# A packed expert table and a rolled expert loop in a two-layer mixture-of-experts kernel

## The reference

```python
_, top_e = lax.top_k(masked, TOP_K)                      # best group of 4 experts, then 2 of its 4
gates = sum over the two of one_hot(top_e, 16) * weight
a = jnp.einsum('bld,edf->blef', h, w1)                   # D 1024 -> 256 for each expert
g = jnp.einsum('bld,edf->blef', h, w3)
hid = jax.nn.silu(a) * g * gates[..., None]
return jnp.einsum('blef,efd->bld', hid, w2)              # 256 -> 1024, summed over experts
```

## Time and profile before

| what | value |
|---|---|
| time, median of 3 runs | 1067.43 us (1067.35 to 1070.24) |
| the profiled execution: time, span | 1068.16 us, 1066.3 us |
| mean granted TensorE clock | 0.886 |
| busy: PE, weight load (PEld) | 800.7 us (75%), 514.3 us (48%) |
| busy: DVE, ACT, POOL | 345.6, 213.9, 123.0 us |
| chain that ended last | PE 60%, DVE 13%, issue 10%, DMA 5% |

### The profile page before, as it was taken

One profiled execution on the slowest core, in us unless ns is written; L12 is line 12 of the kernel. 1 busy time (PEld: TensorE's weight loads), 2 busy tenths in 40 slices (PEclk: granted clock), 3 DMA queues, 4 the chain that ended last, 5 costly groups with the idle time before them and its releaser, 6 DMA issues.

```text
span 1066.3 us, 14079 instructions
## 1 busy us (share of the span) xinstructions
PE 800.7 (75%) x4044; PEld 514.3 (48%) x4044; DVE 345.6 (32%) x756; ACT 213.9 (20%) x513; POOL 123.0 (12%) x181
## 2 busy tenths in 40 slices
PE   4899998789980797867509999977899528987810
PEld 2675554457860353534208655544577514454500
DVE  1102103842757122111064021046527642221126
ACT  1310003542010122222124000044510001222210
POOL 0310100010120010012044000000001110011021
PEclk9999998999975799989758999989999559998965
DMA  9952493783254977897275422328420368569441
GB/s 379 367 219 87 161 415 136 282 354 118 88 209 177 356 242 271 339 386 285 63 286 220 157 80 79 118 70 322 193 79 11 129 241 340 192 220 349 164 142 63
DMA packets 39840, 223.63 MB, mean 210 GB/s; under 512 B 5008, under 2 KB 5840, under 8 KB 22832
## 3 DMA queue, kind: packets, MB, share of 16 engines
q1 hardware_dynamic: 19008, 155.50, 37.6%
q0 software_dynamic: 12240, 50.22, 13.3%
q10 hardware_dynamic: 8480, 16.33, 4.3%
HBM read 194.70 MB, written 27.33 MB: 208 GB/s over the span
## 4 chain that ended last, share of the span: by engine, by line
PE 60%; DVE 13%; issue 10%; DMA 5%; PEld 5%; ACT 3%; PEldq 2%; POOL 1%; ACTq 1%; POOLq 0%; DVEq 0%; SPq 0%
PE psum L499 18%; PE psum L629 7%; PE psum L638 7%; PE psum L496 6%; PE psum L584 4%; PE psum L670 3%; PE psum L659 3%; PEld psum L584 3%; DMA big<-in_weights 3%; PE psum L616 3%; PE psum L448 2%; PE psum L604 2%; DMA shared<-moe_rows,ridx 1%; DVE mxs L1211 1%; PE psum L462 1%
## 5 line engine op out<-in xcount | busy, mean ns | idle before, releaser
L499 PE MATMUL psum<-big 128*128 128x384 f32 x576 | 190.9, 488 | 2.7 <-issue 2.7
L499 PEld LDWEIGHTS psum<-big 128*128 128x128 f32 x576 | 108.6, 190 | 78.6 <-issue 8.3
L638 PE MATMUL psum<-big,shared 128*64 128x256 f32 x576 | 77.4, 428 | 33.3 <-issue 33.3
L1508 DVE TENSOR_SCALAR shared<-shared 128x128 f32<-128x128 f32 (+1 forms) x28 | 7.0, 251 | 258.1 <-ACT shared L1014 258.1
L584 PE MATMUL psum<-big 128*128 128x256 f32 x384 | 83.9, 380 | 2.0 <-ACT big L951 1.8
L629 PE MATMUL psum<-big,shared 128*128 128x512 f32 x160 | 79.6, 656 | 6.3 <-issue 4.0
L584 PEld LDWEIGHTS psum<-big 128*128 128x128 f32 x384 | 72.6, 190 | 12.9 <-issue 3.2
L638 PEld LDWEIGHTS psum<-big,shared 128*64 128x64 f32 x576 | 51.9, 155 | 54.7 <-issue 41.4
L496 PE MATMUL psum<-big 128*128 128x256 f32 x288 | 68.9, 400 | 7.6 <-DMA big<-in_weights 3.9
L448 PE MATMUL psum<-const,big 128*128 128x128 f32 x160 | 31.4, 308 | 51.4 <-ACT big L841 28.0
L496 PEld LDWEIGHTS psum<-big 128*128 128x128 f32 x288 | 57.1, 201 | 18.1 <-ACT big L848 7.5
(11 more groups left out here) (217 smaller groups left out, 912.6 us busy)
## 6 DMA issues: line engine op xcount, KB each, us to landing
big<-in_weights SPq DMA_DIRECT2D x80, 1024.0 KB, 6.9
big<-in_experts SPq DMA_DIRECT2D x22, 2048.0 KB, 11.4
big<-in_experts SPq DMA_DIRECT2D x22, 1024.0 KB, 8.6
moe_rows<-ln_b POOLq DMA_DIRECT2D x3, 3584.0 KB, 25.4
moe_rows<-shared ACTq DMA_DIRECT2D x20, 256.0 KB, 5.9
moe_rows<-shared ACTq DMA_DIRECT2D x36, 128.0 KB, 6.8
ln_b<-in_ln POOLq DMA_DIRECT2D x4, 1024.0 KB, 6.3
gate_b<-mod_rows POOLq DMA_DIRECT2D x4, 1024.0 KB, 7.3
```

The source lines that it names most:

```text
L499: ins = pe.matmul(bank(name)[:, 0:T], w[piece][:, k, part * P:(part + 1) * P], hT[:, k, :], start=(k == 0), stop=(k == KC - 1))
L638: ins = pe.matmul(psD[HALF * j:HALF * j + HALF, 0:DE], xT[:, k * P:k * P + HALF], w[:, 2 * DE * k + DE * j:2 * DE * k + DE * j + DE], star ...
```

## The change

- The start, full and end tables become one number for each expert in use, `end + 4*full + 16*blocks + 64*start` (T_CODE). PE reads one number a stage, SP's buffer waits take it apart too. Unused places hold only a start, so their end is 0.
- PE's sixteen written-out stages become a loop over turns of four stages (one for each weight buffer). Each stage is nested in the one before it and is entered only if the one before it was in use; an expert's further blocks go through one inner loop for full and half blocks. Each turn reads two codes at its start.
- Experts are taken in the order of their number, those in use first. Layer 0 becomes H H FH H, FF H H H, F F H H, H (four turns); layer 1 becomes H H H H, FFF FFH H H, H (three turns).
- DVE: the ops of rank and of blocks by rank go, others for the place of an expert in use come; four ops and the first block's number move ahead of reading the counts; the index is read before the packed table is built, and the table is ready after it.
- POOL: it takes the first block's number from a small tensor of its own (`from_block`), and the first gather is issued directly on the index, without waiting for the table and without the column copy. The loop goes on from the second block.
- SP reads its expert numbers ahead of the waits, ACT reads one packed flag for this block and the one before.

```diff
 # SP
+first_two = [expert(L, r) for r in range(2)]
+for r in range(2):
+    load_up(first_two[r], r)
...
+    e = expert(L, r)
     if r >= BUFS:
-        used = sp.value_load(tabu[0:1, T_START + r - BUFS + 1:...], ...)
+        used = sp.value_load(tabu[0:1, T_CODE + r - BUFS + 1:...], ...) // 64
         sp.wait_ge(up_full, used)
 # PE
-def expert_table(r):
-    load = lambda at, low, high: pe.value_load(tabu[0:1, at + r:at + r + 1], min_val=low, max_val=high)
-    return load(T_START, 1, BLOCKS * DEPTH + 1), load(T_FULL, 0, TILES), load(T_END, 0, 2)
+def expert_code(turn, q):
+    return pe.value_load(tabu[0:1, bass.ds(turn * BUFS + (T_CODE + q), 1)], min_val=0, max_val=MOST)
...
+def stage(L, turn, q, code, end_before):
+    loads = L * (E // BUFS) + turn
+    end, full_blocks = code % 4, code // 4 % 4
+    blocks, start = code // 16 % 4, code // 64
+    w = expert_buffer(q)
+    def down_before():
+        last_down((q - 1) % BUFS, loads + (q > 0), end_before, start)
...
+    with pe.If(end > 0):
+        pe.wait_ge(up_in[q], loads * 16 + 16)
+        up_block(start, full_blocks)
+        following = expert_code(turn, q + 1) if q < BUFS - 1 else None
+        with pe.Fori(0, blocks) as j:
+            i = start + j
+            tokens_T(L, i + 1)
+            with pe.If(j > 0):
+                pe.wait_ge(down_in[q], loads * 16 + 16)
+                down_full_block(i, w)
+            with pe.Else():
+                down_before()
+            with pe.If(full_blocks - j > 0):
+                hidden_T_full(i)
+            with pe.Else():
+                hidden_T_half(i)
+            with pe.If(blocks - j > 1):
+                up_block(i + 1, full_blocks - j - 1)
+        if q < BUFS - 1:
+            stage(L, turn, q + 1, following, end)
+    with pe.Else():
+        down_before()
...
-table, end = expert_table(0), None
-for r in range(E):
-    table, end = stage(L, r, table, end)
+turns = (pe.value_load(tabu[0:1, T_ACTIVE:T_ACTIVE + 1], min_val=1, max_val=E) + (BUFS - 1)) // BUFS
+with pe.Fori(0, turns) as turn:
+    before = expert_code(turn, -1)
+    stage(L, turn, 0, expert_code(turn, 0), before % 4)
+end = expert_code(turns, -1) % 4
 last = pe.value_load(tabu[0:1, T_LAST:T_LAST + 1], min_val=2, max_val=BLOCKS * DEPTH + 1)
-last_down(L, E - 1, end, last)
+last_down(BUFS - 1, L * (E // BUFS) + turns, end, last)
 # ACT
-before, half_block = block_kind(j - 1), block_kind(j)
+half_block, before = block_kinds(j)          # one load, % 2 and // 2
 # DVE, ahead of the counts
+link(dve.tensor_copy(tab[:, T_FIRST:T_FIRST + 1], tab[:, T_LAST:T_LAST + 1]))
+dve.tensor_copy(from_block[:, 0:1], tab[:, T_FIRST:T_FIRST + 1]).then_inc(from_ready, 1)
+# four ops of 3x16 (t16, v16(13)), moved here from behind the first blocks
 # DVE, who and blocks
-link(tt(grid(0, E, 6), cols(tokens, 6), steps, ALU.is_gt)); link(dve.tensor_reduce(halves, ...))
-link(stt(key, ...)); link(tt(grid(0, E, E), rows(key, E), cols(key, E), ALU.is_gt))
-link(dve.tensor_reduce(rank, grid(0, E, E), AX.X, ALU.add))
+link(ts(active, tokens, 0.0, None, ALU.is_gt))
+link(tt(grid(0, E, E), prev, rows(active, E), ALU.mult))
+link(dve.tensor_reduce(place, grid(0, E, E), AX.X, ALU.add))
+link(stt(place, place, 1.0, active, ALU.add, ALU.mult))
...
-link(tt(grid(0, E, E), grid(1, E, E), rows(halves, E), ALU.mult))
-link(dve.tensor_reduce(by_rank, grid(0, E, E), AX.X, ALU.add))
...
-link(tt(grid(0, E, E), grid(1, E, E).rearrange("p r e -> p e r"), rows(base, E), ALU.mult))
-link(dve.tensor_reduce(first_block, grid(0, E, E), AX.X, ALU.add))
...
-link(tt(two, ..., ALU.mult))                  # 2x2x48, then its sum
+link(tt(slots, ..., ALU.mult))                # 2x48, then its sum
 # DVE, behind sel_ready
-# ten ops of the three tables, table_ready, then the index
+# two sums (T_ACTIVE, T_COUNT), the index into gidx (two ops),
+# then halves (two ops), the code (eight ops), by place (two ops of 256),
+# T_LAST, idle places, table_ready
 # POOL
-await_read(pool, L, "index")
+pool.wait_ge(from_ready, L + 1)
+first = pool.value_load(from_block[0:1, 0:1], min_val=1, max_val=BLOCKS * DEPTH + 1)
+def first_gather(b):
+    pool.wait_ge(xT_full, first + L)
+    await_read(pool, L, "index")
+    pool.indirect_dma_start(xg[b], None, h2_d[:, :],
+                            bass.IndirectOffsetOnAxis(gidx[:, 0:1], 0)).then_inc(xg_in[b], 16)
...
 pool.wait_ge(table_ready, L + 1)
-first = pool.value_load(tabu[0:1, T_FIRST:T_FIRST + 1], ...)
 count = pool.value_load(tabu[0:1, T_COUNT:T_COUNT + 1], min_val=1, max_val=BLOCKS)
-with pool.Fori(0, count + 1) as j:
+with pool.Fori(1, count + 1) as j:
```

More of the change, by code:

```diff
@@ L688, in last_down, with up_block @@
                     with pe.Else():
-                        down_full_block(after, expert_buffer(r))
+                        down_full_block(after, expert_buffer(q))
                     stop_here(pe, "pe")
[L692 to L701, removed]
+            def stage(L, turn, q, code, end_before):
[5 more added lines that the diff above has]
+                    last_down((q - 1) % BUFS, loads + (q > 0), end_before, start)
+                def up_block(i, left):
+                    with pe.If(left > 0):
+                        up_full_block(L, i, w)
+                    with pe.Else():
+                        up_half_block(L, i, w)
@@ L1474, in _ @@
-                link(tt(tab[:, T_FULL:T_FULL + E], blocks, half_last, ALU.subtract))
-                link(stt(tab[:, T_END:T_END + E], by_rank, 0.0, half_last, ALU.is_gt, ALU.add))
-                link(dve.tensor_copy(tab[:, T_FIRST:T_FIRST + 1], tab[:, T_LAST:T_LAST + 1]))
-                link(ts(tab[:, T_START:T_START + E], base, tab[:, T_FIRST:T_FIRST + 1], None, ALU.add))
+                await_product(dve, L, "index")
+                src = bank("index")[:, 0:2 * COLS]
+                link(dve.tensor_copy(rt[:, 10, 0:COLS], src[:, COLS:2 * COLS]))
@@ new lines, in _ @@
+                read_out(tt(gidx[:, :], src[:, 0:COLS], rt[:, 10, 0:COLS], ALU.add), "index")
+                link(tt(grid(0, E, 6), cols(tokens, 6), steps.broadcast_to([P, E, 6]), ALU.is_gt))
+                link(dve.tensor_reduce(halves, grid(0, E, 6), AX.X, ALU.add))
+                link(stt(half_last, blocks, 2.0, halves, ALU.mult, ALU.subtract))
+                link(stt(code, base, 4.0, blocks, ALU.mult, ALU.add))
+                link(stt(halves, blocks, 1.0, half_last, ALU.mult, ALU.subtract))
@@ new lines, in _ @@
+                link(stt(code, code, 4.0, halves, ALU.mult, ALU.add))
+                link(stt(halves, active, 1.0, half_last, ALU.mult, ALU.add))
+                link(stt(code, code, 4.0, halves, ALU.mult, ALU.add))
+                link(ts(st[:, 6:7], tab[:, T_FIRST:T_FIRST + 1], 64.0, None, ALU.mult))
+                link(ts(code, code, st[:, 6:7], None, ALU.add))
+                link(tt(grid(0, E, E), grid(1, E, E), rows(code, E), ALU.mult))
+                link(dve.tensor_reduce(tab[:, T_CODE:T_CODE + E], grid(0, E, E), AX.X, ALU.add))
@@ L1478, in _ @@
                 link(tt(tab[:, T_LAST:T_LAST + 1], tab[:, T_FIRST:T_FIRST + 1], tab[:, T_COUNT:T_COUNT + 1], ALU.add))
+                link(ts(st[:, 7:8], tab[:, T_LAST:T_LAST + 1], 64.0, None, ALU.mult))
+                link(ts(idle, num[:, 0:E], tab[:, T_ACTIVE:T_ACTIVE + 1], st[:, 7:8], ALU.is_ge, ALU.mult))
+                link(tt(tab[:, T_CODE:T_CODE + E], tab[:, T_CODE:T_CODE + E], idle, ALU.add))
                 link(dve.tensor_copy(tabu[:, 0:T_WHO], tab[:, 0:T_WHO]))
                 dve.sem_inc(table_ready, 1)
-                await_product(dve, L, "index")
```

143 lines of the change are left out of this document (59 added, 84 removed).

## The result

The changed kernel takes 1061.9 us against 1067.4 us in the median of 20 runs each; the ratio of the runs is 0.9943, 95% interval 0.9928 to 0.9958. Timed again beside the experiments it was 1059.8 us against 1069.0 us, 0.9927 (0.9893 to 0.9962). So it is faster, by 6 to 8 us after these ratios, inside the stated range and on the forecast side, where I had forecast 16 us.

A forecast was written before the change was run, and what follows sets the result against it. PE was taken to bound both loops, losing mostly to issue, and DVE the stretch ahead. Front -5.4, layer 0's loop -9.5 and layer 1's -1.3 sum to -16.2 us, giving 1051.3 us; range 1038 to 1092.

The forecast's parts named there:

- The bound: Both expert loops: PE is the limit, losing mostly to issue, 30.2 us in layer 0 and 18.4 in layer 1.
- the reading of the long gaps: PE's loops: gaps of 4.3 to 5.1 us are waits for instruction pieces, as stage-end branches skip past fetched code.
- Three changes of turn: ... 3.9 us each: Layer 0's loop: each costs 0.9 us, two reads at up to 1 us each, and 1 us to leave and jump back.
- the 1.5 us for fresh code: Each layer's loop: the first turn's code, fetched for the first time, costs about 1.5 us once.
- a sign of being wrong: PE's loops: the prediction is wrong if a change of turn costs over 7 us, or first half blocks wait for weights.
- the 1 us for leaving the nest and jumping back: Part of each change of turn's 3.9 us on PE: leaving four nested branches and jumping back.
- The clock: Layer 0's loop: five long gaps with cold matmuls behind them become four, -2.0 us; layer 1's loop: 0.
- The start's -0.8: Start of each layer's loop: two cold half blocks replace two cold full blocks and a 2.77 us DVE wait, -0.8 us.
- The front: Ahead of each loop: earlier index and gather bring the first transposes forward, -2.7 us a layer, -5.4 us for both.
- Costed at nothing: Both layers: weights issued 1 us later, fewer reads on SP, ACT and DVE, and unused experts were given no cost.
- The jump back: Rival, PE's changes of turn: code is overwritten, so each waits about 8 us; +40, so 1092 us; chance 0.30.
- The changes of expert get no cheaper: Rival, PE's loops: nested branches and inner loop cost what today's skips do; ends at 1066 us; chance 0.15.

The follow-up runs named there:

- turns_out: The changed kernel with its four turns written out one behind the other in place of a loop, no jump back; 1075.2 us, 1.0092 of the kernel before.
- the second execution: The changed kernel profiled once more, unchanged, when timed again beside the experiments; that execution took 1057.4 us.
- late_gather: The changed kernel, but the first gather waits for the packed table as before; 1063.8 us, 0.9952 of the kernel before.
- second_later: The changed kernel, but the second expert's up weights are issued behind the first transposes; 1060.1 us, 0.9936 of the kernel before.
- the first execution: The changed kernel's first profiled execution, 1056.6 us, one of the fastest of its kernel.
- old_stages: The changed kernel with PE's sixteen written-out stages of before, reading the packed code; 1067.5 us, 0.9999 of the kernel before.
- flat_turn: The changed kernel with a turn's four stages one behind the other in place of nested; 1063.5 us, 0.9961 of the kernel before.

## Why the prediction was wrong

**The bound, right; the remedy's own price, wrong.** "Issue" in PE's loop was the thing to cut, and the reading of the long gaps was right: in four of them (427.69, 459.31, 491.67, 969.15) a single branch, line 697 of the kernel before, takes 3.2 to 4.6 us while a piece of instructions comes in (least, median and most of all its branches, in ns):

```profile
L697 PEldq COMPARE_BRANCH  x38: 65/212/4635, 349.9 to 1053.3; - x38
```

Yet issue is still 47.9 of 49.2 us. My terms had it falling by 12.8 (30.2 to 18.6 and 15.0 to 13.8, ACT's waits set apart). The step that failed is "Three changes of turn: ... 3.9 us each", with the 1.5 us for fresh code: five changes and twice the fresh code, 22.5 us in the sum, measured 31.3 us. Two of the five cost over 7 us, which the prediction had named as a sign of being wrong.

The later changes are 0.6 to 1.3 us over the price. The branches and reads of PE in those of layer 0 say where: 1.4 and 2.1 us for the way out of four levels, 0.5 for the jump back, 1.6 for the two reads (up to 2 in the sum), 1.0 and 1.1 for the entry into the next stage (0.9). So the 1 us for leaving the nest and jumping back was too little.

The first change in each layer, 8.2 and 8.6 us, was mis-sized by more than 4 us, and that is again one branch. Of the steps out of the nest (line 712) in layer 0's first change, the last takes 3.1 us, from 397.1 to 400.2, while a piece of instructions comes in (397.9 to 398.8); in layer 0's second change the longest takes 0.17 us and no piece comes in:

```profile
L712 PEldq COMPARE_BRANCH  x5: 92/179/3121, 395.9 to 402.5; - x5
...
L712 PEldq COMPARE_BRANCH  x5: 93/163/169, 452.9 to 456.4; - x5
```

In layer 1's first change it takes 4.1 us. So the change kept, once in a layer, the very wait that it was to remove, a branch over code that has not come in yet; I had put all fresh code of a layer at 1.5 us, by the mean of stages that are stepped through in order. Not all new code does this: turns_out has the wait at the first change (3.5 and 3.9 us) and not at the later ones, where its branches out of the nest take 0.3 us at most though the code is as new. A piece came in 3 to 6 us ahead of those ways out in layer 0 (450.0 and 502.4 us); that this is why is not shown.

**The other 2.7 us of the issue** are the changes within turns and the further blocks: 16.6 us in place of the sum's 9.9 and the 4.0 that the kernel before had ahead of full blocks. The short gaps of the earlier trace rows were the cheapest of their kind; 1.1 to 1.7 us is the usual one here. Nor were there only two sizes before: three changes had gaps of 2.3 to 2.4 us (480.01, 511.54, 989.19).

**The clock** paid part of it back: -5.8 us (-3.3 in the second execution) of busy time, where I had -2.0 for the gaps and, from the blocks of the earlier trace rows, about 1 us more of cold time at each start; the starts took 1.3 and 1.4 us less. (The start's -0.8 in the sum comes out only if 1 us of the 2.77 us for DVE stays, which I did not say; 1.17 us did.) This term rests on how long an execution stays at 1.2 GHz, and it differs by 2.5 us between executions with the same gaps.

**The front:** -1.8 and -2.1 us (-2.0 and -2.3) for the forecast -2.7 each, from the last router matmul to the first transposes. Index and issue were right within 0.5 us; the landing was mis-sized, 8.8 us for the 7.5 that I had chosen between 4.3 and 11.0. The gather's first bytes came 4.3 us after its issue here, beside a weight load, and 1.8 us after it in late_gather, at the tail of one.

**Costed at nothing:** the weights were in time in the changed kernel, where no gap of PE ahead of up matmuls is put down to them. second_later, which issues the second expert's load 11.6 us later, shows that they would not bear that much: the third expert's up matmuls then wait 4.6 and 3.5 us.

**The rivals.** The jump back finds its code: 39 pieces, and 0.24 us at most for the branch. The Trainium skill's sentence on a fetch for each taken branch outside a window of two pages ("Runtime: NRT & Kernel Launch", instruction fetch) is not borne out on PE here as to the window, since a turn of four stages, some six pieces, is fetched once in a layer; that a branch to code not at hand waits agrees with the 3.1 and 4.1 us. The Trainium skill's 128 KB for TensorE ("Advanced Engine Details and Errata", ISA cache) agrees with both lengths of turn: as an estimate from the pieces that came in, a turn of four stages is six of 16.4 KB, 98 KB, and one of eight, which waits 6.2 and 3.9 us at its jump back, ten, 164 KB. So this rival was right about a longer turn than the one it was stated for.

"The changes of expert get no cheaper" came nearest, by the total, though for another reason than the one I gave: they are cheaper within a turn and dear at its end. In all, the two loops gave 4.4 us in the first execution and 1.0 in the second (326.5 less 322.1 and 325.5), and the fronts 3.9 and 4.4: 5 to 8 us, near what the times show. The profiled executions' further 3 and 5 us lie in stretches that the change does not touch. How the gain divides stays open: by these profiles the fronts are about half of it or more, by old_stages, which has the fronts and no gain, they are none.

## What to carry to other kernels

A loop that is rolled up to save instruction fetches pays at its end for what it saves inside: price the way out level by level, the reads, and the first branch over code that has not come in, each by itself, before counting the gaps that go. PE's own branches in the trace, with the pieces that come in beside them, show where a wait for issue goes. Code laid out in the order in which it runs needed no loop here: one nest of sixteen fresh stages took 0.9705 of the time before, where the loop of turns took 0.9943 and 0.9927. And a transfer issued earlier lands earlier only by what the transfers ahead of it leave; what the front gains, the next weights may owe.

## What the runs showed of the hardware

A branch out of PE's nest took 0.17 us in most changes of turn and 3.1 and 4.1 us where a piece of instructions came in meanwhile. The jump back over a loop body of four stages (some six pieces, fetched once in a layer) took 0.08 to 0.24 us, that over one of eight (some ten pieces) 6.2 and 3.9 us at the change of turn. A table read that nothing covered cost 0.75 to 1.0 us.

A gather issued while a weight load is under way moved no byte for 4.3 us; issued at the tail of one it began within 1.9 us, and with the second load held back it landed in 4.3 in place of 8.8 us. DVE was building tables beside it in all three.

Idle time alone does not tell how long the matmuls take: flat_turn's is 1.4 us less than the changed kernel's, in more gaps of 1.5 to 3 us, and its matmuls took 10 to 12 us more, at a granted clock of 0.89 and 0.90 in place of 0.91 to 0.92. That is one execution of the one and two of the other, so how much of it is the gaps' is not shown.
